# A one-core hybrid encoder step on Trainium2: the full-expert branch goes last, the one-hots move to the first expert rounds, the last round is reordered, and half of the row gathers start one expert earlier

## The reference

```python
g_sel = jnp.argmax(g_logits, axis=-1)                 # 1 of 4 groups
top_v, top_i = lax.top_k(e_logits, TOP_K)             # 2 of the 4 experts in it
wts = jax.nn.softmax(top_v, axis=-1) * p_g
eid = g_sel[:, None] * EXPERTS_PER_GROUP + top_i
...
return (jax.nn.silu(xi @ w_gate[e]) * (xi @ w_up[e])) @ w_down[e]
...
x = x + hmoe(rms_norm(x, p['norm_ffn']), ...)         # each token gets 2 weighted expert rows
y = rms_norm(x, norm_final)
```

## Time and profile before

| | us |
|---|---|
| median of three runs | 1055.69 |
| lowest and highest | 1054.32, 1058.29 |
| the profiled execution, its own time | 1055.09 |
| its span, first to last instruction | 1053.3 |

### The profile page before, as it was taken

How to read it: one execution, slowest core, us unless ns; L and a number is a source line. 1 busy time by engine, 2 the same in 40 slices (tenths; PEclk the granted TensorE clock), 3 DMA queues, 4 the chain that set the end, 5 groups by cost and what they waited for, 6 DMA issues and landing times.

```text
span 1053.3 us, 16974 instructions
## 1 busy us (share of the span) xinstructions
PE 1011.3 (96%) x6950; PEld 899.4 (85%) x6950; DVE 666.0 (63%) x1009; ACT 539.7 (51%) x719; POOL 162.5 (15%) x178
## 2 busy tenths in 40 slices
PE   6999999999999999999999999999999999999984
PEld 4999899998999888888988998787788888888863
DVE  5334753453223366767665666466888989898976
ACT  5236533432223335455575633233588888878853
POOL 2111100000000123332321010031201010101061
PEclk9999999999999999999999999999999999999988
DMA  7877865527355475575363280527999999999765
GB/s 184 201 215 176 164 140 65 96 45 114 58 66 111 106 122 64 81 69 64 101 221 121 70 275 27 214 101 299 413 412 413 413 415 412 415 412 415 315 128 150
DMA packets 126172, 207.55 MB, mean 197 GB/s; under 512 B 11230, under 2 KB 68574, under 8 KB 126099
## 3 DMA queue, kind: packets, MB, share of 16 engines
q1 hardware_dynamic: 110290, 149.38, 52.4%
q0 software_dynamic: 13168, 47.59, 13.2%
q10 hardware_dynamic: 2640, 9.57, 2.3%
HBM read 174.40 MB, written 32.12 MB: 196 GB/s over the span
## 4 chain that ended last, share of the span: by engine, by line
PE 82%; DVE 5%; DMA 5%; ACT 4%; issue 3%; POOL 1%; DVEq 0%; POOLq 0%; ACTq 0%
PE ps L1222 22%; PE ps L1224 22%; PE ps L1223 22%; PE ps L1198 5%; DMA x<-y_rows,rows_i 2%; PE ps L1380 2%; PE ps L1394 2%; DMA x_rows<-h,slot_i 1%; PE ps L1356 1%; ACT w_hi L835 1%; PE ps L1340 1%; PE ps L1495 1%; PE ps L1355 1%; PE ps L1292 1%; DMA xg<-x_rows 1%
## 5 line engine op out<-in xcount | busy, mean ns | idle before, releaser
L1935 DVE TENSOR_TENSOR e_lo<-raw,e_hi 128x2048 fp32r<-128x2048 f32 x96 | 219.3, 2288 | 28.5 <-ACT e_hi L1015 28.4
L1015 ACT ACTIVATE e_hi<-raw 128x2048 fp32r<-128x2048 f32 x96 | 184.0, 1918 | 54.9 <-PE ps L1224 43.9
L1222 PE MATMUL ps<-h_hi,w_hi 128*128 128x272 f32 x632 | 186.7, 295 | 0.0
L1224 PE MATMUL ps<-h_hi,w_lo 128*128 128x272 f32 x632 | 182.3, 288 | 0.0
L1223 PE MATMUL ps<-h_lo,w_hi 128*128 128x272 f32 x632 | 181.9, 288 | 0.0
L1721 DVE TENSOR_TENSOR w_lo<-ring,w_hi 128x2048 fp32r<-128x2048 f32 (+1 forms) x40 | 72.5, 1812 | 80.1 <-ACT w_hi L835 80.1
L835 ACT ACTIVATE w_hi<-ring 128x1024 fp32r<-128x1024 f32 (+1 forms) x56 | 79.6, 1421 | 80.1 <-PE ps L1224 72.6
L1222 PEld LDWEIGHTS ps<-h_hi,w_hi 128*128 128x128 f32 x632 | 119.1, 188 | 1.2 <-issue 0.7
L1223 PEld LDWEIGHTS ps<-h_lo,w_hi 128*128 128x128 f32 x632 | 119.1, 188 | 0.2
L1224 PEld LDWEIGHTS ps<-h_hi,w_lo 128*128 128x128 f32 x632 | 118.8, 188 | 0.0
L1222 PE MATMUL ps<-w_hi,h_hi 128*128 128x256 f32 x384 | 110.0, 287 | 2.6 <-DVE va L2006 2.6
(11 more groups left out here) (432 smaller groups left out, 2040.4 us busy)
## 6 DMA issues: line engine op xcount, KB each, us to landing
raw<-in_w_gate_dram SPq DMA_DIRECT2D x32, 1024.0 KB, 10.8
raw<-in_w_up_dram SPq DMA_DIRECT2D x32, 1024.0 KB, 9.6
raw<-in_w_down_dram SPq DMA_DIRECT2D x32, 1024.0 KB, 9.8
ring<-in_w_in_dram SPq DMA_DIRECT2D x24, 1024.0 KB, 10.6
x_rows<-zero POOLq DMA_DIRECT2D x16, 512.0 KB, 7.6
ring<-in_w_in_dram SPq DMA_DIRECT2D x16, 512.0 KB, 8.4
xg<-x_rows POOLq DMA_DIRECT2D x15, 512.0 KB, 6.2
y_rows<-yo ACTq DMA_DIRECT2D x14, 512.0 KB, 6.5
```

The source lines that it names most:

```text
L1015: act.activation(e_hi[buf][:], raw[slot][:], ACT.Copy).then_inc(s_ehi, 1)
L1222: pe.matmul(out, left[0], right[0], start=first, stop=False)
L1224: return pe.matmul(out, left[1], right[0], start=False, stop=final)
L1935: dve.tensor_tensor(e_lo[slot][:], raw[slot][:], e_hi[buf][:].bitcast(F32), ALU.subtract).then_inc(s_elo, 1)
```

## The change

- **Gathers.** Rows of y_rows are shifted by one, with row 0 as the zero row. `rows_index` sorts each token's two rows into a lower and a higher one, and puts the zero row for what is absent; a token whose lower row is expert 13's takes it as its higher one. The five gathers of the lower rows read experts 0 to 12 only (EARLY) and wait for expert 12's store alone. They stand on POOL ahead of `slot_weight(15)`. The five of the higher rows follow, and wait for expert 13's store.
- **One-hots.** The four small instructions and the first half of hot are made in round 1, the second half in round 2, each before the fourth part of the round on DVE.
- **The last round.** On DVE `gated` stands before L4, and hl_lo before L5; on ACT `silu` before L4 and hl_hi before L5; on PE the transposes of hot stand between L4 and L5.
- **The tail.** `overflow` moves into the branch, and the branch behind the finishes, the squares and the stores of the output. On DVE each finish follows the add of the next tile. The value n_ovf is written in round 0. The branch now has its own second pass of squares, finishes and stores.

```diff
             slot_weight(NE - 2)
-            slot_weight(NE - 1)
             pool.wait_ge(s_ovi, 1)
             pool.wait_ge(s_yst[0], 16 * LAST // 2)
+            pool.wait_ge(s_yst[1], 16 * (LAST // 2 - 1))
+            for i in range(NTILE):
+                add_rows(i, 0, rows_i, s_rows[i], y_rows[0:EARLY + 1])
+            slot_weight(NE - 1)
             pool.wait_ge(s_yst[1], 16 * LAST // 2)
-            add_rows(0, 0, rows_i, s_rows[0])
             for i in range(NTILE):
-                if i + 1 < NTILE:
-                    add_rows(i + 1, 0, rows_i, s_rows[i + 1])
                 pool.wait_ge(s_rows[i], 48)
                 add_rows(i, 1, rows_i, s_rows[i])
...
             part_hi(third_after(r, 0, 1))
             h_out(r - 1)
-            for j in range(1, 4):
+            for j in range(1, 3):
                 part_hi(third_after(r, j, 1))
             silu(r, part_of(r, 3, 1))
-            part_hi(third_after(r, 4, 1))
+            part_hi(third_after(r, 3, 1))
             act.wait_ge(s_at, NE)
             act.activation(hl_hi[:].rearrange("p c t -> p (c t)"), ps[:, 2], ACT.Copy).then_inc(s_hhi, 1)
+            part_hi(third_after(r, 4, 1))
             act.wait_ge(s_part, part_of(r, 5, 1)[0] + 1)
...
-            pe.wait_ge(s_into, 4)
+            pe.wait_ge(s_hlo, NE)
+            last_down(part_of(NE, 4), 4)
+            pe.wait_ge(s_into, 5)
             transposes(P, [(ps[:, (3, 0)[k], P * i:P * i + P], hot[:, k, i]) for k in range(2) for i in range(NTILE - 1)], s_hot)
             transposes(TS, [(ps[:, 1, TS * k:TS * k + TS], hot[0:TS, k, NTILE - 1]) for k in range(2)], s_hot)
-            pe.wait_ge(s_hlo, NE)
-            last_down(part_of(NE, 4), 4)
             last_down(part_of(NE, 5), 5)
...
                 step(dve.tensor_tensor_scan(ov[:, 3], ones[:, 0:NE], ov[:, 2], 0.0, ALU.mult, ALU.add))
+                dve.wait_ge(s_ovi, 1)
+                dve.tensor_copy(ovi[:, 0:1], ov[:, 3, NE - 1:NE]).then_inc(s_ovi, 1)
...
+                step(dve.scalar_tensor_tensor(y_slot, y_slot, 1.0, away, ALU.add, ALU.add))
+                low, high = home[:, 0:NTILE], home[:, NTILE:2 * NTILE]
+                step(dve.tensor_tensor(low, y_slot[:, 0:NTILE], y_slot[:, NTILE:2 * NTILE], ALU.min))
+                step(dve.tensor_tensor(high, y_slot[:, 0:NTILE], y_slot[:, NTILE:2 * NTILE], ALU.max))
+                step(dve.tensor_scalar(away[:, 0:NTILE], low, float(EARLY), float(4 * NE * CAP), ALU.is_le, ALU.mult))
+                step(dve.tensor_tensor(away[:, 0:NTILE], low, away[:, 0:NTILE], ALU.add))
+                step(dve.tensor_tensor(high, high, away[:, 0:NTILE], ALU.min))
+                step(dve.scalar_tensor_tensor(rows_i[:, 0:NTILE], low, float(EARLY), low, ALU.is_le, ALU.mult))
+                dve.scalar_tensor_tensor(rows_i[:, NTILE:], high, float(LATE), high, ALU.is_le, ALU.mult).then_inc(s_ovi, 1)
...
+            def last_one_hots(k):
+
+                if k == 0:
+                    dve.wait_ge(s_sc[0], 96)
+                    two = [ybase[:, 2 + q].rearrange("p (e i) -> p e i", e=2) for q in range(2)]
+                    dve.wait_ge(s_ovi, 1)
+                    step(dve.tensor_tensor(ybase[:, 1, 0:NTILE], slot_f[:, 0], slot_f[:, 1], ALU.subtract))
+                    step(dve.tensor_tensor(two[0], onehot[:, 0, :, LAST:NE].rearrange("p i e -> p e i"), rep(ybase[:, 1, 0:NTILE], 1, 2), ALU.mult))
+                    step(dve.tensor_tensor(two[1], two[0], rep(slot_f[:, 1], 1, 2), ALU.add))
+                    step(dve.tensor_tensor(two[0], two[1], rep(iota_r[:, LAST:NE], 2, NTILE), ALU.subtract))
+                dve.tensor_tensor(hot[:, k], rep(iota_s[:], 1, NTILE), rep(ybase[:, 2, NTILE * k:NTILE * k + NTILE], 2, CAP),
                                   ALU.is_equal).then_inc(s_into, 1)
...
                 part_lo(third_after(r, 2, odd))
+                if isinstance(r, int) and r in (1, 2):
+                    last_one_hots(r - 1)
                 part_lo(third_after(r, 3, odd))
                 gated(r, odd)
...
             h_out(r - 1)
-            part_lo(third_after(r, 1, 1))
-            last_one_hots()
-            for j in range(2, 4):
+            for j in range(1, 3):
                 part_lo(third_after(r, j, 1))
             gated(r, 1)
-            part_lo(third_after(r, 4, 1))
+            part_lo(third_after(r, 3, 1))
             dve.wait_ge(s_hhi, NE)
             dve.tensor_tensor(hl_lo[:].rearrange("p c t -> p (c t)"), ps[:, 2], hl_hi[:].bitcast(F32).rearrange("p c t -> p (c t)"),
                               ALU.subtract).then_inc(s_hlo, 1)
+            part_lo(third_after(r, 4, 1))
             dve.wait_ge(s_y, NE - 1)
             y_kept(NE - 2, 0, 2)
-            overflow()
             dve.wait_ge(s_y, NE)
             y_kept(NE - 1, 0, 1)
             dve.wait_ge(s_y, NE + 1)
             y_kept(NE - 1, 1, 1)
...
+            dve.wait_ge(s_gf, 16)
+            add(0)
+            for i in range(1, NTILE):
+                add(i)
+                finish(i - 1, 0)
+            finish(NTILE - 1, 0)
             n_ovf = dve.value_load(ovi[0:1, 0:1], min_val=0, max_val=NOVF)
             with dve.If(n_ovf > 0):
+                dve.wait_ge(s_out[0], 48)
+                dve.wait_ge(s_out[1], 32)
+                overflow()
...
-            def finish(i):
-                n = TILES[i][1]
-                dve.wait_ge(s_fsq, i + 1)
-                step(dve.reciprocal(stat[0:n, 55 + i:56 + i], stat[0:n, 55 + i:56 + i]))
-                dve.scalar_tensor_tensor(fo[0:n, i], x2[0:n, i], stat[0:n, 55 + i:56 + i], gfin[0:n], ALU.mult, ALU.mult).then_inc(s_fo, 1)
-
-            dve.wait_ge(s_gf, 16)
-            for i in range(NTILE):
-                finish(i)
```

97 lines of the change are left out of this document (54 added, 43 removed).

## The result

The changed kernel takes 1048.71 us (median of five runs, 1046.08 to 1050.19) against 1055.69 us (1054.32 to 1058.29). The ratio is 0.9916, 95% interval 0.9894 to 0.9938: about 9 us faster by the ratio, 7.0 us by the medians. The profiled execution took 1050.19 us with a span of 1048.4 us, 1.5 us above the median. The forecast was 1046.0 us with a range of 1044.3 to 1048: the time lies 0.7 us above that range and inside the wide one, 1043.0 to 1050.0.

What follows compares the result with a forecast made beforehand. Gathers, PE and DVE's adds were taken to end together near 1039. Terms 4.1 + 2.5 + 0.8 + 4.0 - 1.0 - 0.7 = 9.7 us off 1055.09 gave 1045.4, median 1046.0; range 1044.3 to 1048, wide 1043.0 to 1050.0.

Steps and rivals of the forecast that it cites:

- The last round: Last round on PE: without waiting for hh and at full clock, PE ends L5 at 1023.0, 6.6 us earlier.
- 4.1 us of waiting: Last round: without the one-hots and one e_lo ahead of hh on DVE, `AT` moves from 1017.08 to 1013.0, 4.1 us.
- 2.5 us of clock: Last round, from `AT` to the end of the next part: 3.21 us instead of 5.71 at low clock, 2.5 us.
- overflow: After L5: DVE's last x_lo no longer comes behind `overflow`, so PE does not wait for it, 0.8 us.
- The tail: First add to end of last finish: alternating adds and finishes takes 13.4 us instead of 17.4, 4.0 us.
- The gathers as cover: Low gathers from about 991.7, high ones from 1008.6 at latest, last landed by 1028: adds never wait, 6 us spare.
- The rival that they stay the bound: Gathers share DMA engines with the last weights and still land at 1038.8: 1050.9 us, chance 0.12.
- The jump behind the last work: End of span: DVE and SP jump after their last work, minus 0.7 us, bounds 0 and 2.8.
- The early one-hots: Added work in rounds 1 and 2: PE stalls 0.8 and 0.2 us, minus 1.0 us, bounds 0 and 2.4.
- The one-hots cost the clock too: Rival: a stall in round 1 or 2 drops PE to 1.2 GHz, 2.5 us each: 1051.0 us, chance 0.08.
- The low gathers hold the queue: Rival: five low gathers go only one after another, 8.28 us each: about 1085 us, chance 0.03.
- POOL keeps DVE out: Rival: each of five low gathers holds DVE for 2.94 us: 1058.8 us, chance 0.03.

Runs made afterwards that it cites:

- the kernel that waits 4.02 us again: The kernel before with only the gathers' and indices' part of the change: median 1056.5 us, ratio 0.9999.
- both runs that had one: The changed kernel with the one-hots back in the last round, 1050.58 us (0.9934), and with the old order of the last round, 1049.96 us (0.9939).
- the pair of runs: The changed kernel with gathers back behind expert 13's store, 1055.13 us (0.9983); the kernel before with the gathers' move alone, 1056.5 us (0.9999).
- the second profile after: Profile of the changed kernel run again, unaltered: span 1045.3 us, no slow matmuls; median 1047.39 us, ratio 0.9918.
- the first experiments: Include the changed kernel run again unaltered, ratio 0.9918; 21 runs of the kernel before beside it had spans of 1052.3 to 1058.6 us.
- the second group: The changed kernel again, unaltered, beside new runs of the kernel before: median 1047.39 us, ratio 0.9918.
- POOL's passes over long vectors: The changed kernel with one-hots in round 0 and one finish on POOL, 1045.7 us (0.9903), or two finishes off DVE, 1047.85 us (0.9913).

## Why the prediction was right, and where it was off

**The last round was right to 0.1 us.** hh at 1016.97 (row: 1017.01), `AT` at 1018.07 (1018.03), the first add at 1026.1 on the old time line, so 7.4 us earlier; measured 7.43. The parts: 4.1 us of waiting, shown by 1.82 and 2.28 us for its two halves; 2.5 us of clock, shown by a PEclk of 1.00 in the windows after and 0.60 in the kernel that waits 4.02 us again. The prediction tied the 2.5 us to the wait for hh. That a half of this wait was followed by full clock, in both runs that had one, was not in it; it did not matter here, since the whole wait went.

**overflow**, 0.8: the first add came 7.43 us earlier, and 4.1 + 2.5 + 0.8 = 7.4. Put back alone it costs 1.37. The two do not clash: in the kernel before PE waited 0.62 us behind it, in the changed one with `overflow` put back 1.12 us.

**The tail**, 4.0: measured 17.42 - 13.56 = 3.86, and 17.33 again with the branch in the middle. The two waits of DVE that it named, 0.3 and 0.1, are 0.42 and 0.15.

**The gathers as cover** held: no add waits for one. The forecast of the pace was too slow for the low ones (2.2 us each in the mean and 0.3 between, 2.94 was the bound) and about right for the first issue. The high ones began 1.8 us later than the forecast's latest time (1015.43 - 5.07 = 1010.4 against 1008.6), because expert 13's store landed only after 7.9 us, not 6.5; the spare time took it up. Also, the prediction's ten gathers in 33.2 us before are nine: the tenth, issued at 1034.52, landed at 1039.79. The rival that they stay the bound fell; in the other direction the pair of runs shows how much hung on them, 5.6 us.

**The jump behind the last work**, -0.7, was mis-sized: the end behind the last finish is 3.74 us instead of 3.1, and the runs with and without the branch price it at 1.4 us. The step that failed: the forecast let the span end with the jump. The jump itself ends where it said, 3.11 us behind the last finish (1047.77 - 1044.66), and 0.6 us of closing work follow. It was inside its bounds of 0 and 2.8.

**The early one-hots**, -1.0, cost about 1.1 us: 0.75 ahead of round 2 (0.8 forecast) and 0.2 to 0.5 in the lead (0.2 forecast), which is 216.30 to 216.49 us in the seven profiles that have them in rounds 1 and 2 and 215.97 to 216.10 in the three that have them in the last round. With them in round 0 it is 216.03 to 216.20: by the means of the groups they cost 0.1 us there.

**What the sum lacked** is the scatter ahead of 760 us. Against the profile before, the second profile after is 8.0 us shorter: 9.95 us won in the stretch, 1.25 us lost by the one-hots (0.76, and 0.49 in the lead of this pair), and 0.7 us lost with the rows of expert 1, which landed 0.64 us later. The first profile lost another 3 us by the clock. The sum of 9.7 against a single profile took that profile's early rounds for the kernel's; it had no slow matmul there, while its runs spread over 4 us, and by the 21 runs beside the first experiments over 6. So the median after lies 2.7 us above the forecast: 0.6 us by the jump, 0.1 to 0.25 by the one-hots, 0.1 by the tail, and the remaining 1.8 us is less than this scatter. Eleven runs of the changed kernel together have a median of 1047.69 us, and in the second group the medians lie 9.0 us apart (1047.39 against 1056.40). That the total came so near is thus partly luck; the parts behind expert 12's store are what the runs bear out.

**The rivals.** "The one-hots cost the clock too" predicted such a loss, 2.5 us. It is not the one: in the first profile the low clock ends at 756.9, before the first one-hot, and the second profile has the one-hots and no low clock. The stall ahead of round 2 was followed by full clock in all seven profiles that have it. The reason given against this rival, that 0.8 us is short, does not carry as a rule: the 7 or 8 slow matmuls in six profiles follow a longest wait of 0.62 to 1.64 us. "The low gathers hold the queue" fell: the five landed 2.7 us apart (1004.42 to 1015.35), with up to four under way at once. "POOL keeps DVE out" fell for what it was meant for: e_lo stays at 2.29 us in round 14 with POOL at work for 7.2 us. The Trainium skill ("SBUF — State Buffer", "Who interferes with whom") has the lock work both ways. For the gathers the trace shows it again one way, POOL's issue taking 2.2 to 3.1 us beside DVE's e_lo and 1.35 to 1.55 beside an idle one. For POOL's passes over long vectors it shows the other way in two of three overlaps: 1.74 and 1.93 us for a finish of 1.28. The finish was slowed there and not shut out for the whole of POOL's pass, as the lock would have it: the one of 1.74 us ended 0.67 us before the pass did. That the adds with one operand in PSUM stay at 1.21 to 1.23 agrees with the Trainium skill's rule (same section) that an instruction with one SBUF input does not contend.

## What to carry to other kernels

When several things end together, an experiment that undoes one part and one that does it alone can give 5.6 and 0.2 us, and both are true; price the parts from the trace in which the others are already done. Measure from a mark behind the noise (here the store of expert 12) rather than by medians: the mark gave 0.1 us where single runs scatter by 4 to 6. A branch whose body never runs still costs the jump over it, here 2.6 us in the middle of DVE's work and 1.4 behind the last of it, where SP's own jump ends last, and before more is cut from a tail that ends in stores one should look at how they queue.
